# Moving the first two weight splits of a two-group encoder trunk: one behind the eviction of the modulation rows, one to GpSimd

## The chip, the cores and the metric

The kernel runs on one core of one Trainium2 chip. The metric is the device time of one execution in microseconds (us); lower is better. Engines are named as in the profile: PE is TensorE (PEld its weight loads), DVE is VectorE, ACT is ScalarE, POOL is GpSimd, SP is the engine whose queue issues the DMAs. "L543" is line 543 of the kernel before.

## The reference, cut to what matters

Two request groups of 512 tokens by 1024 features each go through the same two-layer encoder trunk. Each layer normalises, mixes and adds; only the start of layer 0 matters here.

```python
def trunk(x, c, g_norm, w_ada, b_ada, g_final, even_p, odd_p):
    for l in range(DEPTH):
        mod = jax.nn.silu(c) @ w_ada[l] + b_ada[l]
        shift, scale, gate = jnp.split(mod, 3, axis=-1)
        h = rmsnorm(x, g_norm[l]) * (1 + scale[:, None, :]) + shift[:, None, :]
        ...
        out = even_mixer(h, ...)          # layer 0: begins with u = h @ w_in0
        x = x + gate[:, None, :] * out
    return rmsnorm(x, g_final)
```

So before the first large product `h @ w_in0` can start, the kernel needs the modulation rows (`mod`), the norm of x, and h made from both.

## The kernel before

**Number format.** All large products are done in three passes to keep float32 accuracy: a weight block w is split into `w_hi` (w rounded to the type fp32r) and `w_lo` = w - `w_hi`, the activations likewise into `h_hi` and `h_lo`, and PE does `w_hi*h_hi`, `w_hi*h_lo`, `w_lo*h_hi` (L561, L562, L563 in `three`). The weights come as 81 blocks of 128 x 1024 per group. SP loads them into a ring of three slots (`wring`, L556); for each block ACT rounds it (`act_split`, L531, semaphore `w_hi`) and DVE subtracts (`dve_split`, L543, semaphore `w_lo`), into two pairs of buffers. PE waits on `w_lo` before it uses a block (`wait_split`), and SP loads block n+3 once `w_lo` has counted n+1.

**The prologue.** Before the first block, DVE and PE fold small weights together (`expand` L441, `keep` L446 to L448, `fold` L368 to L372), PE accumulates the modulation rows of the first of three parts over eight steps (`ada_step`, L303) as their weights arrive, ACT squares x (L637), POOL adds the squares (`n_gpsimd`, L644 and L647), PE sums them over partitions (L652) and ACT makes `rstd` (L658, L660). Then ACT rounds the weight blocks 0 and 1 (L531).

**The end of the prologue on DVE, in program order.** `ada_evict` copies the modulation rows out of the accumulator bank (L319); `ada_add` waits for four transposes of them on PE (L311), adds the bias (L328) and makes the two scale rows (L334, twice). Then `dve_h` makes h in eight chunks of 128 x 512: for chunk c an instruction at L588 (x times scale times `rstd`, semaphore `h_scaled`), on ACT the rounding and shift (`act_h`, L599, semaphore `h_hi`), on DVE again the low half (L593, semaphore `h_lo`). The order is: L588 of chunk c, then L593 of chunk c-1. `dve_h` takes a table `splits`, by which the split of block 0 stands ahead of chunk 1 and that of block 1 ahead of chunk 2:

```python
        groups[0].dve_h(dve, 0, 0, h_A, xT, splits={1: 0, 2: 1})
```

**What PE does first.** `pe_project_two` works on blocks 0 and 1 together, in 16 steps of three matmuls. The steps are (block 0, chunk 0), (1, 0), (0, 1), (1, 1) and so on to chunk 5, then (0, 6), (0, 7), (1, 6), (1, 7). Chunk k waits for `h_lo` of that chunk; chunk 0 of block 0 waits for `w_lo` to count 1, chunk 0 of block 1 for 2. After that the blocks are done one by one; the block after next is split by ACT when a block is done.

**Orders.** Each engine runs a program of its own, written out by hand, and they meet only at semaphores. POOL's program is `n_gpsimd`, then `a_gpsimd` of group 0, whose first wait is for the constants and the bias tables.

Of the kernel before, what the change touches and what calls it, by code (L numbers as in the profile page):

```python
# [5 lines left out]
F32 = mybir.dt.float32  # L6
F32R = mybir.dt.float32r
ALU = mybir.AluOpType
# [36 lines left out]
for _n, _w in (("ident", P), ("blk", 32), ("ones", P), ("mf", 1), ("mb", 1), ("eps", 1), ("one", 1), ("mhalf", 1), ("pad", 3),  # L45
# [13 lines left out]
SLOTS = 3  # L59
PAIRS = 2  # L60
# [11 lines left out]
    up_in=32, w_lo=81, x_back=16, x_gfin=8, x_out=16, x_upd=16, y_hi=8, y_lo=8, z_bias=0, z_in0=128, z_in1=128, z_norm=3,  # L72
    z_out0=128, z_out1=128, z_sg=16)

Group = namedtuple("Group", "a_sync a_gpsimd a_tensor a_scalar a_vector e_sync e_gpsimd e_tensor e_scalar e_vector act_split dve_split stream_weights"
                           " dve_h act_h n_square n_gpsimd n_tensor n_rstd fin_tensor fin_rstd fin_scale fin_out")


# [5 lines left out]
def trunk(nc, xs, rows_in, fold_in, w_ada, blocks_in, up_q, up_kv, rpb_pad, const_in, out):  # L84
# [7 lines left out]
    def sem(name):  # L92
        if name not in sems:
            sems[name] = nc.alloc_semaphore(name)
        return sems[name]
# [7 lines left out]
    def take(n, at=None):  # L103
        lo = free[0] if at is None else at
        if at is None:
            free[0] += (n + 7) // 8 * 8
        assert lo + n <= 53200, (lo, n)
        return nc.alloc_sbuf_tensor_at(f"at_{lo}_{n}", [P, n], F32, offset=arena_at + 4 * lo)[:, :]

    def chunks(ap, w):  # L110
        return ap.rearrange("p (c w) -> p c w", w=w)

    def take_r(name, n, at=None):

        lo = free[0] if at is None else at
        if at is None:
            free[0] += n
        assert lo + n <= 53200, (name, lo, n)
        return nc.alloc_sbuf_tensor_at(name, [P, n], F32R, offset=arena_at + 4 * lo)[:, :]
# [3 lines left out]
    def cst(name, rows=P):  # L123
        a, b = CONST[name]
        return const[0:rows, a:b]
# [13 lines left out]
    xT = chunks(take(DC * T), T)  # L139
# [4 lines left out]
    whi = take_r("w_hi", PAIRS * DC * P).rearrange("p (s k n) -> p s k n", s=PAIRS, k=DC)  # L144
    wlo = take_r("w_lo", PAIRS * DC * P).rearrange("p (s k n) -> p s k n", s=PAIRS, k=DC)
    ring_lo = free[0]
    wring = take(SLOTS * DC * P).rearrange("p (s k n) -> p s k n", s=SLOTS, k=DC)
# [18 lines left out]
    def pair(name, hi_at, lo_at, n=DC):  # L166
        return (chunks(take_r(name + "_hi", n * T, at=hi_at), T), chunks(take_r(name + "_lo", n * T, at=lo_at), T))
# [57 lines left out]
    h_A = pair("h_a", Q0, K0)  # L225
# [36 lines left out]
    def ps(n):  # L262
        return PS[n // 2][:, n % 2 * T:n % 2 * T + T]
# [19 lines left out]
    groups = []  # L283
# [30 lines left out]
    def ada_evict(dve, p):  # L314

        dve.wait_ge(sem("ada_used"), DC * (p + 1))
        if p:
            dve.wait_ge(sem("ada_T"), p)
        dve.tensor_copy(ada_rows, ps(ADA_BANK[p])).then_inc(sem("ada_ev"), 1)  # L319

    def ada_add(dve, p):

        dve.wait_ge(sem("ada_T"), p + 1)
        lo = VA["bada"][0] + 2 * DC * p
        o = mod.rearrange("p l c g -> p (l c) g")[:, 2 * DC * p:2 * DC * (p + 1)].rearrange("p (q n) g -> p q n g", q=4)
        src = ps(TURN_BANK[p]).rearrange("p (n q r) -> p q n r", n=4, q=4)[:, :, :, 0:G]
        bias = vecA[:, lo:lo + 2 * DC].rearrange("p (q n) -> p q n", q=4).unsqueeze(3).to_broadcast([P, 4, 4, G])
        dve.tensor_tensor(o, src, bias, ALU.add).then_inc(sem("mod_set"), 1)  # L328
        if p != 1:
            l = p // 2  # L330
            dve.wait_ge(sem("mod_set"), 5 if l else 1)
            at_gn = VA["gn"][0] + DC * l
            for g in range(G):
                dve.scalar_tensor_tensor(scl[:, l, :, g], mod[:, l, DC:2 * DC, g], 1.0, vecA[:, at_gn:at_gn + DC], ALU.add, ALU.mult)\  # L334
                    .then_inc(sem("mod_set"), 1)
# [93 lines left out]
    def p_vector(dve):  # L429

        dve.memset(ps(ADA_BANK[0]), 0.0).then_inc(sem("p_zero"), 1)
        dve.memset(Weff.rearrange("p c x -> p (c x)"), 0.0).then_inc(sem("p_zero"), 1)
        dve.wait_ge(sem("p_vecT"), 1)
        dve.tensor_copy(vecA, ps(0)[:, 0:P]).then_inc(sem("p_vec"), 1)
        dve.tensor_copy(vecB, ps(0)[:, P:2 * P]).then_inc(sem("p_vec"), 1)
        blk = cst("blk").unsqueeze(2).to_broadcast([P, 32, 4])

        def expand(c):
            for w in range(3):
                a = Araw[:, w, c, :].unsqueeze(1).to_broadcast([P, 32, 4])  # L440
                dve.tensor_tensor(X[:, w, c, :].rearrange("p (n i) -> p n i", i=4), a, blk, ALU.mult).then_inc(sem("p_X"), 1)  # L441

        def keep(c):
            dve.wait_ge(sem("p_fold"), c + 1)
            b = ps(FOLD_BANKS[c])
            dve.tensor_copy(Gt[:, c], b[:, 0:P]).then_inc(sem("p_folded"), 1)  # L446
            dve.tensor_copy(BDv[:, c], b[:, P:2 * P]).then_inc(sem("p_folded"), 1)
            dve.tensor_copy(Weff[:, 2 * c:2 * c + 2, 0:16], b[:, 2 * P:2 * P + 32].rearrange("p (a n) -> p a n", a=2))\  # L448
                .then_inc(sem("p_folded"), 1)

        dve.wait_ge(sem("p_raw"), 16)
        dve.tensor_copy(bif, fold_src[:, FOLD_BIF:FOLD_W])
        dve.wait_ge(sem("p_zero"), 2)
        for c in range(6):
            expand(c)
        for c in range(F_LATE):
            keep(c)
            if c + 6 < IC:
                expand(c + 6)
        ada_evict(dve, 0)  # L460
        ada_add(dve, 0)
        dve.wait_ge(sem("mod_set"), 3)
        dve.wait_ge(sem("rstd_done"), 1)
        groups[0].dve_h(dve, 0, 0, h_A, xT, splits={1: 0, 2: 1})

    def by_col(ap):

# [44 lines left out]
    def group(g):  # L512
# [20 lines left out]
        def dve_split(dve, b):  # L533

            n = B_END * g + b
            if n >= B_END * G:
                return
            dve.wait_ge(sem("w_hi"), n + 1)
            if b == B_KR:
                dve.tensor_tensor(whi[:, n % PAIRS, :, ROPE:2 * ROPE], wring[:, n % SLOTS, :, 0:ROPE],  # L540
                                  whi[:, n % PAIRS, :, 0:ROPE].bitcast(F32), ALU.subtract).then_inc(sem("w_lo"), 1)
                return
            dve.tensor_tensor(wlo[:, n % PAIRS], wring[:, n % SLOTS], whi[:, n % PAIRS].bitcast(F32), ALU.subtract)\  # L543
                .then_inc(sem("w_lo"), 1)

        def pair_of(b):

            return (B_END * g + b) % PAIRS
# [278 lines left out]
        def a_vector(dve):  # L827

            for b in range(B_OUT0):
# [13 lines left out]
                if B_NAQK <= b < B_NAV:  # L843
# [7 lines left out]
                    else:  # L851
                        dve.tensor_tensor(nak[1][:, n - 4], ps(b % 4), nak[0][:, n - 4].bitcast(F32), ALU.subtract)\
                            .then_inc(sem("naqk_lo"), 1)
                dve_split(dve, b + PAIRS)
                if B_GATE + 1 <= b < B_GATE + 5:
                    for e in range(2):
# [1042 lines left out]
        def e_vector(dve):  # L1899
# [168 lines left out]
            for b in range(B_TAIL + 2, B_END):  # L2068
# [7 lines left out]
                if half:  # L2076
# [1 line left out]
                    dve.scalar_tensor_tensor(xT[:, j], ps(j), mod[:, 1, 16 + j, g:g + 1], xT[:, j],  # L2078
                                             ALU.mult, ALU.add).then_inc(sem("x_upd"), 1)

        return Group(a_sync, a_gpsimd, a_tensor, a_scalar, a_vector, e_sync, e_gpsimd, e_tensor, e_scalar, e_vector, act_split, dve_split,
                     stream_weights, dve_h, act_h, n_square, n_gpsimd, n_tensor, n_rstd, fin_tensor, fin_rstd, fin_scale, fin_out)

    groups.extend(group(g) for g in range(G))
    LAST = groups[G - 1]

    with nc.Block() as block:

        @block.sync
        def _(sp):  # L2090
            p_sync(sp)
            for group_ in groups:
                group_.a_sync(sp)
                group_.e_sync(sp)
            for j in range(DC):
                LAST.fin_out(sp, j)
            sp.wait_ge(sem("y_out"), 16 * DC * G)

        @block.gpsimd
        def _(pool):  # L2100
            groups[0].n_gpsimd(pool)
            for group_ in groups:
                group_.a_gpsimd(pool)
                group_.e_gpsimd(pool)

        @block.tensor
        def _(pe):
            p_tensor(pe)
            for group_ in groups:
                group_.a_tensor(pe)  # L2110
                group_.e_tensor(pe)
            LAST.fin_tensor(pe, 6)

        @block.scalar
        def _(act):
            p_scalar(act)
            for group_ in groups:
                group_.a_scalar(act)
                group_.e_scalar(act)
            LAST.fin_rstd(act, 6)  # L2120

        @block.vector
        def _(dve):
            p_vector(dve)
            for group_ in groups:
                group_.a_vector(dve)
                group_.e_vector(dve)
            for j in range(DC):
                LAST.fin_scale(dve, j)
# [143 lines left out]
```

## Time and profile before

| what | value |
|---|---|
| median of 3 runs | 1488.36 us (1488.08 to 1489.69) |
| time of the profiled execution | 1488.46 us |
| its span, first to last instruction | 1486.4 us |
| mean granted PE clock | 0.997 |
| PE busy | 1449.8 us (98%) |
| DVE busy | 854.4 us (57%) |
| ACT busy | 669.9 us (45%) |
| POOL busy | 365.2 us (25%) |

Times within the profile are us from the start of the span. An instruction's row gives its start, its duration, the engine, the line and the operands; in square brackets stands how long the engine had been idle before it and what released it. Instructions follow each other on an engine a little before the end of the one ahead as it is shown, since they are pipelined.

### The profile page before, as it was taken

The numbers are of one execution on the slowest core, as the hardware profiler recorded it, in microseconds if no ns is written. First come the engines' busy times: TensorE is split into PE (matmuls) and PEld (weight loads), VectorE is DVE, ScalarE is ACT, GpSimd is POOL, SyncE is SP. The second block draws the span as 40 slices with busy tenths as digits, with TensorE's granted clock in tenths as the row PEclk, the third lists the DMA queues.
The fourth block names the chain that finished last, engine by engine and source line by source line (L and its number), as shares of the span: only waits on it lengthen the run. The fifth ranks groups of instructions, "written<-read, shape, count | busy, mean of one in ns | idle before, by whom it ended". The sixth has DMA issues, their size and how long they took to land.

```text
span 1486.4 us, 18893 instructions
## 1 busy us (share of the span) xinstructions
PE 1449.8 (98%) x7162; PEld 1115.2 (75%) x7162; DVE 854.4 (57%) x1523; ACT 669.9 (45%) x1161; POOL 365.2 (25%) x455
## 2 busy tenths in 40 slices
PE   8999999999999999999999999999999999999997
PEld 5677765678787787787888887567878778787885
DVE  7523345655797427885443434566689652789423
ACT  3323446744443435543543343765444343555332
POOL 2011023421100022765210002342120002376311
PEclk9999999999999999999999999999999999999999
DMA  9566732214333331116334544222433333111531
GB/s 385 203 221 214 256 128 86 58 57 142 107 99 100 95 111 57 44 29 240 88 97 160 133 119 111 96 58 58 142 111 100 95 107 106 50 43 31 183 99 71
DMA packets 54618, 174.27 MB, mean 117 GB/s; under 512 B 6000, under 2 KB 7408, under 8 KB 52224
## 3 DMA queue, kind: packets, MB, share of 16 engines
q1 hardware_dynamic: 54528, 173.07, 36.0%
q8 instruction: 57, 0.93, 0.3%
q14 instruction: 33, 0.27, 0.1%
HBM read 149.94 MB, written 23.10 MB: 116 GB/s over the span
## 4 chain that ended last, share of the span: by engine, by line
PE 82%; DVE 8%; ACT 4%; DMA 2%; issue 2%; POOL 1%; SPq 0%; DVEq 0%; ACTq 0%; POOLq 0%
PE ps L561 21%; PE ps L563 21%; PE ps L562 21%; PE ps L1115 3%; PE ps L1151 2%; PE ps L1170 2%; PE ps L1658 1%; PE ps L1641 1%; DVE w_lo L543 1%; PE ps L303 1%; PE ps L1692 1%; PE ps L1189 1%; PE ps L1482 1%; PE ps L1132 1%; DMA at<-z_kept 1%
## 5 line engine op out<-in xcount | busy, mean ns | idle before, releaser
L543 DVE TENSOR_TENSOR w_lo<-at,w_hi 128x1024 fp32r<-128x1024 f32 x160 | 199.1, 1244 | 345.2 <-ACT w_hi L531 345.1
L531 ACT ACTIVATE w_hi<-at 128x1024 fp32r<-128x1024 f32 x162 | 169.5, 1047 | 140.1 <-PE ps L563 130.6
L561 PE MATMUL ps<-h_e_hi,w_hi 128*128 128x512 f32 x464 | 182.8, 394 | 5.0 <-DVE w_lo L543 5.0
L563 PE MATMUL ps<-h_e_hi,w_lo 128*128 128x512 f32 x464 | 180.6, 389 | 0.0
L562 PE MATMUL ps<-h_e_lo,w_hi 128*128 128x512 f32 x464 | 180.6, 389 | 0.0
L561 PE MATMUL ps<-h_a_hi,w_hi 128*128 128x512 f32 x384 | 153.7, 400 | 1.6 <-DVE h_a_lo L593 1.0
L562 PE MATMUL ps<-h_a_lo,w_hi 128*128 128x512 f32 x384 | 150.1, 391 | 0.0
L563 PE MATMUL ps<-h_a_hi,w_lo 128*128 128x512 f32 x384 | 150.0, 391 | 0.0
L561 PEld LDWEIGHTS ps<-h_e_hi,w_hi 128*128 128x128 f32 x464 | 87.1, 188 | 28.8 <-issue 8.7
L563 PEld LDWEIGHTS ps<-h_e_hi,w_lo 128*128 128x128 f32 x464 | 87.1, 188 | 18.3
L562 PEld LDWEIGHTS ps<-h_e_lo,w_hi 128*128 128x128 f32 x464 | 87.1, 188 | 18.0 <-issue 0.5
L1300 POOL TENSOR_SCALAR at<-at,at 128x256 f32<-128x256 f32 (+1 forms) x128 | 76.0, 611 | 98.9 <-DVE at L1250 98.9
L561 PE MATMUL ps<-u_h_hi,w_hi 128*128 128x512 f32 x256 | 100.2, 391 | 0.0
L563 PE MATMUL ps<-u_h_hi,w_lo 128*128 128x512 f32 x256 | 99.6, 389 | 0.0
L562 PE MATMUL ps<-u_h_lo,w_hi 128*128 128x512 f32 x256 | 99.6, 389 | 0.0
L1468 DVE SCALAR_TENSOR_TENSOR at<-ps,at,at 128x510 f32<-128x510 f32 (+1 forms) x128 | 95.9, 749 | 4.5
L561 PEld LDWEIGHTS ps<-h_a_hi,w_hi 128*128 128x128 f32 x384 | 72.4, 188 | 29.8 <-issue 12.0
L1569 POOL TENSOR_TENSOR at<-at,at 128x512 f32<-128x512 f32 x16 | 22.2, 1412 | 284.9 <-DMA at<-a_rows 284.9
L563 PEld LDWEIGHTS ps<-h_a_hi,w_lo 128*128 128x128 f32 x384 | 72.4, 188 | 15.4
L562 PEld LDWEIGHTS ps<-h_a_lo,w_hi 128*128 128x128 f32 x384 | 72.5, 189 | 14.8 <-issue 0.7
L573 POOL TENSOR_TENSOR at<-at,at 128x512 f32<-128x512 f32 x25 | 38.1, 1525 | 138.1 <-ACT at L1895 95.0
L1234 DVE TENSOR_REDUCE at<-ps 128x2 f32<-128x1024 f32 x32 | 39.2, 1225 | 42.8 <-PE ps L1115 42.8
(289 smaller groups left out, 3007.0 us busy)
## 6 DMA issues: line engine op xcount, KB each, us to landing
at<-blocks_in SPq DMA_DIRECT2D x162, 512.0 KB, 3.8
at<-w_ada SPq DMA_DIRECT2D x32, 512.0 KB, 4.6
at<-w_ada SPq DMA_DIRECT2D x8, 1024.0 KB, 17.7
at<-xs SPq DMA_DIRECT2D x4, 2048.0 KB, 10.7
z_kept<-at SPq DMA_DIRECT2D x32, 256.0 KB, 2.1
at<-z_kept SPq DMA_DIRECT2D x32, 256.0 KB, 2.7
sg_kept<-at SPq DMA_DIRECT2D x16, 256.0 KB, 4.5
at<-sg_kept SPq DMA_DIRECT2D x16, 256.0 KB, 2.6
```

Source lines behind the costliest of these rows:

```text
L531: act.activation(whi[:, n % PAIRS, :, cols], wring[:, n % SLOTS, :, cols], ACT.Copy).then_inc(sem("w_hi"), 1)
L543: dve.tensor_tensor(wlo[:, n % PAIRS], wring[:, n % SLOTS], whi[:, n % PAIRS].bitcast(F32), ALU.subtract)\
L561: pe.matmul(o, stationary[0], moving[0], start=first, stop=False)
L562: pe.matmul(o, stationary[0], moving[1], start=False, stop=False)
L563: return pe.matmul(o, stationary[1], moving[0], start=False, stop=final)
L573: pool.tensor_tensor(acc, acc, sqb[:, c % 2], ALU.add).then_inc(sem("sq_added"), 1)
L1115: last = pe.matmul(ps(s_bank(j) + e), qcat[0:QK, u, m * P:(m + 1) * P], kcat[0:QK, u], start=True, stop=True)
L1151: last = pe.transpose(ps(4 + q)[:, col:col + P], Pt[:, j % 4, m, k * P:(k + 1) * P], ident)
L1170: last = pe.matmul(ps(6 + n % 2)[64 * e:64 * e + 64, 2 * P * half:2 * P * half + 2 * P], vmla[:, s, 2 * n + e], PT[(j - 1 + e) % 4][:, 2 * ...
L1234: dve.tensor_reduce(nmx[:, 2 * i:2 * i + 2], ps2(i % 2).rearrange("p (e t) -> p e t", e=2), AX.X, ALU.max, negate=True).then_inc(sem("c_ma ...
L1300: last = pool.tensor_scalar(p, p, rinv[:, n:n + 1], 1.0, ALU.mult, ALU.mult)
L1468: dve.scalar_tensor_tensor(y[:, lo:hi], src[:, lo + d:hi + d], vb("convw", t * IC + c), y[:, lo:hi], ALU.mult, ALU.add).then_inc(sem("e_co ...
```

## The change

Block 0 is now split on DVE directly behind the eviction of the modulation rows, ahead of the bias add. Block 1 is split by POOL, with the same subtraction of a 128 x 1024 block, behind the norm's additions and ahead of the bias tables; POOL waits for `w_hi` to count 2 and for `w_lo` to count 1. `dve_h` no longer holds any split. Later splits stay as they were.

```diff
         ada_evict(dve, 0)
+        groups[0].dve_split(dve, 0)
         ada_add(dve, 0)
         dve.wait_ge(sem("mod_set"), 3)
         dve.wait_ge(sem("rstd_done"), 1)
-        groups[0].dve_h(dve, 0, 0, h_A, xT, splits={1: 0, 2: 1})
+        groups[0].dve_h(dve, 0, 0, h_A, xT)
...
+        def pool_split(pool, b):
+
+            pool.wait_ge(sem("w_hi"), b + 1)
+            pool.wait_ge(sem("w_lo"), b)
+            pool.tensor_tensor(wlo[:, b % PAIRS], wring[:, b % SLOTS], whi[:, b % PAIRS].bitcast(F32), ALU.subtract)                .then_inc(sem("w_lo"), 1)
...
         @block.gpsimd
         def _(pool):
             groups[0].n_gpsimd(pool)
+            groups[0].pool_split(pool, 1)
             for group_ in groups:
                 group_.a_gpsimd(pool)
                 group_.e_gpsimd(pool)
```

(The rest of the diff adds `pool_split` to the tuple of functions that `group` returns.)

## Rows read from the trace of the kernel before

**Rows 1.** The page, part 1: busy time and share of the span.
```profile
PE 1449.8 (98%) x7162; PEld 1115.2 (75%) x7162; DVE 854.4 (57%) x1523; ACT 669.9 (45%) x1161; POOL 365.2 (25%) x455
```

**Rows 2.** Chain that ended last, around 37: start, us, what.
```profile
37.01 1.13 DVE w_lo L543
```

**Rows 3.** Timeline of DVE: start, us, engine, line, operands, idle before.
```profile
34.19 0.69 DVE L319 COPY at<-ps 128x512 f32<-128x512 f32 x1 [0.41 <-PE ps L303]
35.75 0.19 DVE L328 TENSOR_TENSOR at<-ps,at 128x32 f32<-128x32 f32 x1 [0.87 <-PE ps L311]
35.98 0.24 DVE L334 SCALAR_TENSOR_TENSOR at<-at,at 128x8 f32<-128x8 f32 x2
36.26 0.75 DVE L588 SCALAR_TENSOR_TENSOR at<-at,at,at 128x512 f32<-128x512 f32 x1
36.92 1.22 DVE L543 TENSOR_TENSOR w_lo<-at,w_hi 128x1024 fp32r<-128x1024 f32 x1
38.06 0.74 DVE L588 SCALAR_TENSOR_TENSOR at<-at,at,at 128x512 f32<-128x512 f32 x1
38.72 0.74 DVE L593 SCALAR_TENSOR_TENSOR h_a_lo<-at,at,h_a_hi 128x512 fp32r<-128x512 f32 x1
39.38 1.22 DVE L543 TENSOR_TENSOR w_lo<-at,w_hi 128x1024 fp32r<-128x1024 f32 x1
40.52 0.74 DVE L588 SCALAR_TENSOR_TENSOR at<-at,at,at 128x512 f32<-128x512 f32 x1
41.18 0.74 DVE L593 SCALAR_TENSOR_TENSOR h_a_lo<-at,at,h_a_hi 128x512 fp32r<-128x512 f32 x1
...
48.42 1.63 DVE L593 SCALAR_TENSOR_TENSOR h_a_lo<-at,at,h_a_hi 128x512 fp32r<-128x512 f32 x2
```

**Rows 4.** Timeline of ACT, same stretch.
```profile
33.77 1.06 ACT L531 ACTIVATE w_hi<-at 128x1024 fp32r<-128x1024 f32 x1 [3.21 <-DMA at<-blocks_in]
35.06 1.06 ACT L531 ACTIVATE w_hi<-at 128x1024 fp32r<-128x1024 f32 x1 [0.23 <-DMA at<-blocks_in]
37.04 0.72 ACT L599 ACTIVATE h_a_hi<-at,at 128x512 fp32r<-128x512 f32 x1 [0.93 <-DVE at L588]
```

**Rows 5.** Timeline of PE, first three-pass products.
```profile
39.61 0.76 PE L561 MATMUL ps<-h_a_hi,w_hi 128*128 128x512 f32 x1 [0.98 <-DVE h_a_lo L593]
...
42.31 0.45 PE L561 MATMUL ps<-h_a_hi,w_hi 128*128 128x512 f32 x1
...
52.05 0.39 PE L563 MATMUL ps<-h_a_hi,w_lo 128*128 128x512 f32 x1
...
54.83 0.39 PE L561 MATMUL ps<-h_a_hi,w_hi 128*128 128x512 f32 x1
...
64.80 0.39 PE L563 MATMUL ps<-h_a_hi,w_lo 128*128 128x512 f32 x1
```

**Rows 6.** Windows: stretch, us, busy PE PEld DVE ACT POOL, clock, DMA share, GB/s.
```profile
38.10:38.70 0.60, 0.53 (x5) 0.43 (x4) 0.60 (x2) 0.00 (x0) 0.00 (x0) 1.00 0.15 62
38.70:39.60 0.90, 0.00 (x0) 0.02 (x1) 0.90 (x3) 0.72 (x1) 0.00 (x0) 0.68 0.88 153
39.60:42.30 2.70, 2.69 (x6) 2.04 (x7) 2.67 (x4) 1.00 (x4) 0.00 (x0) 0.50 0.63 208
```

**Rows 7.** Timeline of POOL and of DVE near 696.
```profile
695.90 1.29 POOL L1588 TENSOR_TENSOR at<-at,at 128x512 f32<-128x512 f32 x1 [0.20 <-DMA at<-z_kept]
696.16 2.12 DVE L543 TENSOR_TENSOR w_lo<-at,w_hi 128x1024 fp32r<-128x1024 f32 x1 [1.78 <-ACT w_hi L531]
```

**Rows 8.** Windows of L441 alone: stretch, us, busy DVE, clock, DMA share, GB/s.
```profile
17.09:19.57 2.48, 2.48 (x3) 1.00 1.01 420
...
26.88:27.56 0.68, 0.68 (x3) 1.00 1.02 422
```

**Rows 9.** Groups of POOL by shape, and its timeline at 93.
```profile
L1560 POOL TENSOR_TENSOR xc_g_lo<-at,xc_g_hi 128x512 fp32r<-128x512 f32 x32 | 41.1, 1284 | 2.6
```
```profile
93.53 1.33 POOL L761 TENSOR_TENSOR at<-at,at 128x256 f32<-128x256 f32 x2 [8.25 <-DMA t_masked<-at]
```

More of the change, by code:

```diff
@@ L73 @@
     z_out0=128, z_out1=128, z_sg=16)
-Group = namedtuple("Group", "a_sync a_gpsimd a_tensor a_scalar a_vector e_sync e_gpsimd e_tensor e_scalar e_vector act_split dve_split stream_weights"
+Group = namedtuple("Group", "a_sync a_gpsimd a_tensor a_scalar a_vector e_sync e_gpsimd e_tensor e_scalar e_vector act_split dve_split pool_split stream_weights"
                            " dve_h act_h n_square n_gpsimd n_tensor n_rstd fin_tensor fin_rstd fin_scale fin_out")
@@ L2079, in e_vector @@
                                              ALU.mult, ALU.add).then_inc(sem("x_upd"), 1)
-        return Group(a_sync, a_gpsimd, a_tensor, a_scalar, a_vector, e_sync, e_gpsimd, e_tensor, e_scalar, e_vector, act_split, dve_split,
+        return Group(a_sync, a_gpsimd, a_tensor, a_scalar, a_vector, e_sync, e_gpsimd, e_tensor, e_scalar, e_vector, act_split, dve_split, pool_split,
                      stream_weights, dve_h, act_h, n_square, n_gpsimd, n_tensor, n_rstd, fin_tensor, fin_rstd, fin_scale, fin_out)
```

## The prediction

> **What bounds the kernel now.** I read the page first: PE is busy in 98% of the span [rows 1], so the time moves only where PE waits or runs at its lower clock. Then the chain of waits: nearly all of it is the three-pass matmuls, and at the end of the prologue it leaves PE for DVE, through the split of block 0 [rows 2]. The edit is all in that place, so I read the timelines of DVE, ACT and PE from 34 to 53. The reader is to see four things.
>
> First, DVE is idle for 0.87 between the eviction, which ends at 34.88, and the bias add at 35.75, and there is no idle time on it from there to 50.05 that matters [rows 3]: 34.88 to 35.75 is the hole in which the first split is to go. Second, the rounded block 0 is there at 33.77 + 1.06 = 34.83 and block 1 at 36.12 [rows 4]. Third, PE stands idle for 0.98 before its first three-pass matmul at 39.61, 0.15 behind the first `h_lo` (38.72 + 0.74 = 39.46) [rows 3, 5]. Fourth, PE's granted clock falls in that hole, from 1.00 to 0.50, the lower of its two levels (1.2 against 2.4 GHz), and stays there to about 42.3 [rows 6]: the first six matmuls of the pair take 42.31 - 39.61 = 2.70, 0.45 each, and the other 42 take 52.28 - 42.31 = 9.97 [rows 5], where 52.28 is the last start plus 0.23. In block 2's even stretch the 4th starts at 54.83 and the 48th at 64.80, 44 steps of 0.2266 [rows 5], which makes 9.52 for 42; the missing 0.45 is waiting for DVE, whose last `h_lo` comes at 50.05, with nine matmuls (2.23) behind it.
>
> **The change part by part.**
>
> *Two splits leave `dve_h`.* Each costs DVE 1.14 there (36.92 to the next start, 38.06; 39.38 to 40.52) [rows 3]. That alone would bring the last `h_lo` 2.28 earlier.
>
> *Split of block 0 behind the eviction.* It needs the rounded block 0, there at 34.83, and DVE, free at 34.88 [rows 3, 4]: from 34.88 to 36.10 (1.22). The bias add behind it can start at about 36.02 in place of 35.75: +0.27. The hole hides 0.87 of the 1.14. PE's four transposes wait for the eviction only and don't move. The cover is thin: the block is there 0.05 before it is needed, where it had 36.92 - 34.83 = 2.09 to spare; whatever the block lands later is now paid in full (third rival).
>
> *Split of block 1 on POOL.* The trace has no POOL subtraction of 128 x 1024. The nearest is L1560, the same operation with the same output type on 128 x 512, 1.284; the bias tables at 256 columns take 1.33 for two, 0.67 each [rows 9]. The slope between them is (1.284 - 0.67)/256, 2.4 ns a column, so 1024 columns come to 1.284 + 512 x 0.0024 = 2.51. Bounds: 2 x 1.284 = 2.57, and 4.3 if it is held up as much in proportion as DVE's split there [rows 7] was (2.12 for 1.22, 2.5 x 1.74). I take 2.5. It starts when `w_lo` counts 1 (36.10) and `w_hi` 2 (36.12); ACT starts 0.03 behind a DVE release (37.04 behind 37.01) [rows 3, 4], so I put POOL at 36.15 to 36.2, and its end at 38.7. Behind it in POOL's queue stand only the bias tables, whose data SP asks for no sooner than at its fifth block, long after: free. PE needs this half only three matmuls after its first: also free. SP issues block 3 behind the first split, which ends at 36.10 in place of 38.14, and block 4 behind the second, 38.7 in place of 40.60 [rows 3]; neither block is needed before the pair and block 2 are through PE, so nothing is gained or lost.
>
> *What POOL's split does to DVE.* This is the price that decides. POOL runs a two-input add from 695.90 to 697.19 [rows 7]; DVE's split, the same that takes 1.22 elsewhere, starts at 696.16 and ends at 698.28, 1.09 behind POOL's end: DVE did nothing while POOL ran. The multiplies of the prologue say it again: three `expand` multiplies take 0.68 together when POOL is quiet and 2.48 when POOL adds squares [rows 8], 1.80 of waiting. So a DVE instruction with two operands in SBUF waits out a POOL instruction that started first. In the changed kernel DVE issues such instructions from 36.25 on (L334 takes `mod` and the norm weights; L588 takes x and `rstd`), POOL starts at 36.15 to 36.2, and all of DVE stands until 38.7. The bias add of L328 has one operand in PSUM and is through by 36.2.
>
> The Trainium skill ("SBUF — State Buffer", "Who interferes with whom") states the same as a rule: the shared port pair is an exclusive lock, a DVE instruction with two SBUF inputs contends with a GpSimd instruction that reads SBUF, and whoever issues first makes the other block fully. By that rule the sum is the one below; by its absence the first rival's. On the size of POOL's part the skill ("GPSIMD Engine Reference", "Performance versus the Vector engine") gives 4497 ns for a tensor_tensor add of 2048 columns; half of that, an estimate, is 2.25, and the stall would be 0.25 shorter. The rows of this kernel, 1.284 for 512, decide for 2.5.
>
> *The sum on DVE.* POOL ends at 38.7. The two L334 are through by 38.9, and L588 of chunk 0 starts at 38.93 (36.26 before). L588 of chunk 1 follows 0.66 later, at 39.6. ACT rounds chunk 0 from 38.93 + 0.75 + 0.03 = 39.71 to 40.43; L593 of chunk 0 waits for that and runs from 40.46 to 41.20. So the first `h_lo` comes at 41.20, 1.74 later than 39.46. L588 of chunk 2 starts at 41.24 in place of 40.52, and from there the rhythm is that of before: each further `h_lo` is 0.72 later, the last at 50.77. In short: +0.27 for what of split 0 sticks out of the hole, +2.4 for the stall, -2.28 for the two splits, and +0.3 since L593 of chunk 0 now waits for ACT, which the split of block 0 used to cover.
>
> *The sum on PE.* Its folds still end at 38.6. It starts at 41.20 + 0.15 = 41.35, idle 2.7 where it was 0.98. The clock falls in the hole as before. If it comes back as long after PE's restart as in the rows (2.70), six matmuls run to 44.05 and 42 at 0.2266 to 53.6; DVE is ahead throughout (the 40th matmul, which needs the last `h_lo`, would start at 51.6, after 50.77). Before it was 52.28: +1.3. If the clock comes back at the same moment as before, 42.3, DVE's last `h_lo` sets the end: 50.77 + 2.23 = 53.0, +0.7. I take +1.3, since the row at the lower level shows PE at work for nearly all of it [rows 6]; the +0.7 is the lower end.
>
> Everything later hangs on this: the next block's ACT split waits for the first block's end, DVE's for that, PE for that, and the prologue's end is not hidden behind any load. So the +1.3 goes through to the end, and nothing else in the program changes. Span 1486.4 + 1.3 = 1487.7; the profiled execution's time of 1488.46 would become 1489.8, and against the median of 1488.36, 0.10 below that execution, I forecast 1489.7.
>
> **The rivals.** About 0.2%, 3.0 us, is what a measurement here can tell from no change.
>
> *POOL and DVE run side by side (other sign, faster).* Place: DVE from 36.2 to 38.7. Without the stall L588 of chunk 0 starts at 36.53, the first `h_lo` comes at 38.80, the last at 48.4, PE starts at 38.95: 38.95 + 2.70 + 9.52 = 51.2, so -1.1 and 1487.3. It decides if POOL's instruction delays DVE by less than 1.1 of its 2.5. For it: nothing but that POOL might be woken late, and even then one L588 gets ahead of it and the others wait. Against it: [rows 7, 8]. I give it 0.10.
>
> *The clock stays low for longer (slower).* PE's hole is 2.7 in place of 0.98. Each us more at 1.2 GHz costs 1 - 0.2266/0.45 = 0.50, 0.45 being the slow step above. If the low stretch behind the restart is 4.4, +0.8 more, so +2.1 and 1490.5; twice the row, 5.4, gives +2.6 and 1491.0. It passes 0.2% only if the low level holds for 6.1 behind the restart. For it: the stall itself; against: the row shows one rise and no case of a longer one. 0.17, of it 0.03 beyond +3.0.
>
> *The blocks land late (slower).* ACT idles for both blocks' DMAs [rows 4]; every us that block 0 lands later than here now delays the bias add and all behind it. One block's place in the queue is 1.29 (35.06 - 33.77): +1.3 on top, +2.6 and 1491.0. It decides from 0.05 on; it takes 1.7 to pass 0.2%. 0.08, of it 0.03 beyond.
>
> *The gain or loss is swallowed later* (a load or another engine is waited for anyway): 1488.4, 0.07.
>
> **How the numbers follow.** Forecast with its bounds (+0.7 to +2.1, 1489.0 to 1490.5): 0.58. The five cases make 1.00. The predicted time is 1489.7. The range takes in the side-by-side case and the two slower ones up to +2.9: 1487.2 to 1491.3; outside it I leave some 0.10 and the scatter of the runs, of which three spread over 1.6. Faster by over 0.2% (below 1485.4) no case gives: 0.03 for what I haven't seen. Slower by over 0.2% (above 1491.3): 0.03 + 0.03, and 0.02 for a slower POOL instruction (4.3 in place of 2.5 makes 1.3 + 1.8 = +3.1): 0.08. Within: 0.89.
>
> **What the profile after would show.** A DVE split at 34.9 and the bias add near 36.0; one POOL subtraction at 36.2, 2.5 long; behind it an L334 or L588 on DVE whose duration is stretched by the overlap; the first L593 near 40.5 and the last ending near 50.8; PE idle for about 2.7 before its first L561 at 41.3; the last matmul of the pair at about 53.4. Wrong would be: L588 at its 0.75 within POOL's instruction (then faster), a low clock beyond 45, or a w_hi of block 0 later than the eviction.

## The result, and the profile after

The changed kernel takes 1491.3 us (median of 22 runs, 1489.0 to 1497.58); the kernel before takes 1488.57 (22 runs beside them, 1487.03 to 1491.12). The ratio is 1.0016, 95% interval 1.001 to 1.0023: slower by 2.4 us, clear of zero (1.5 to 3.4), and less than the 0.2% (3.0 us) that was named as the bound of "no change", though the interval reaches past it. The profiled execution took 1490.73, with a span of 1488.9 against 1486.4.

The timeline of DVE after, at the end of the prologue (columns as ahead of the prediction; L588 is now L595, L593 is L600, L543 is L544, and the three matmuls are L568 to L570):

```profile
34.07 0.69 DVE L319 COPY at<-ps 128x512 f32<-128x512 f32 x1 [0.41 <-PE ps L303]
34.68 1.22 DVE L544 TENSOR_TENSOR w_lo<-at,w_hi 128x1024 fp32r<-128x1024 f32 x1
35.81 0.18 DVE L328 TENSOR_TENSOR at<-ps,at 128x32 f32<-128x32 f32 x1
36.03 2.41 DVE L334 SCALAR_TENSOR_TENSOR at<-at,at 128x8 f32<-128x8 f32 x2
38.48 1.42 DVE L595 SCALAR_TENSOR_TENSOR at<-at,at,at 128x512 f32<-128x512 f32 x2
40.02 0.75 DVE L600 SCALAR_TENSOR_TENSOR h_a_lo<-at,at,h_a_hi 128x512 fp32r<-128x512 f32 x1
40.80 0.75 DVE L595 SCALAR_TENSOR_TENSOR at<-at,at,at 128x512 f32<-128x512 f32 x1
...
48.72 1.63 DVE L600 SCALAR_TENSOR_TENSOR h_a_lo<-at,at,h_a_hi 128x512 fp32r<-128x512 f32 x2
```

The timeline of POOL, and of ACT, in the same stretch:

```profile
36.04 2.38 POOL L551 TENSOR_TENSOR w_lo<-at,w_hi 128x1024 fp32r<-128x1024 f32 x1 [10.95 <-DVE w_lo L544]
```
```profile
32.97 1.06 ACT L532 ACTIVATE w_hi<-at 128x1024 fp32r<-128x1024 f32 x1 [2.53 <-DMA at<-blocks_in]
34.26 1.06 ACT L532 ACTIVATE w_hi<-at 128x1024 fp32r<-128x1024 f32 x1 [0.23 <-DMA at<-blocks_in]
39.26 1.39 ACT L606 ACTIVATE h_a_hi<-at,at 128x512 fp32r<-128x512 f32 x2 [3.94 <-DVE at L595]
```

The two L334 of 128x8, which took 0.24 [rows 3], take 2.41, from 36.03 to 38.44. POOL's subtraction runs from 36.04 to 38.42: 0.02 from end to end, though neither waits for a semaphore of the other there. Taken apart, the first L334, whose record starts 0.01 ahead of POOL's, takes 0.17 as before; the second, from 36.11 to 38.44, is the one that stands.

PE's timeline at the first, seventh and last matmul of the pair, and the windows around its hole (columns as before):

```profile
40.91 0.76 PE L568 MATMUL ps<-h_a_hi,w_hi 128*128 128x512 f32 x1 [2.41 <-DVE h_a_lo L600]
...
43.61 0.50 PE L568 MATMUL ps<-h_a_hi,w_hi 128*128 128x512 f32 x1
...
53.02 0.39 PE L570 MATMUL ps<-h_a_hi,w_lo 128*128 128x512 f32 x1
```
```profile
38.50:40.40 1.90, 0.01 (x1) 0.00 (x0) 1.77 (x3) 1.14 (x2) 0.00 (x0) 1.00 0.93 272
40.40:43.60 3.20, 2.69 (x6) 2.15 (x7) 3.13 (x5) 1.94 (x6) 0.00 (x0) 0.50 0.30 118
```

PE idles for 2.41 in place of 0.98 [rows 5], and six matmuls run at the lower clock, as before; the low stretch itself is 3.4 long in both traces. To compare kernels whose prologues end some tenths apart, I take the distance from the start of the eviction (L319) to the start of the pair's last matmul: 52.05 - 34.19 = 17.86 before [rows 3, 5], 53.02 - 34.07 = 18.95 after, +1.09.

That is not the whole of +2.4. I followed the start of each block's split through both traces. The shift is +0.98 behind the pair (53.67 against 52.69) and +1.31 at 188; +0.38 at 349, and -0.13 at 912. Between 188 and 349 the profile of before was long by chance: all 13 other profiles made here are 0.1 to 1.3 shorter there. For the 0.5 between 349 and 912 I have no account. Then, in the attention of group 2, nothing of which was edited, it jumps to +2.52 at 1027 and stays near there to the end (+2.22). At that place stand DVE's timeline and POOL's, of the kernel before and then of the changed one:

```profile
918.63 0.68 DVE L973 TENSOR_TENSOR at<-ps,at 32x512 f32<-32x512 f32 x1 [4.99 <-DMA sg_kept<-at]
...
920.05 0.70 DVE L977 TENSOR_TENSOR at<-at,at 32x512 f32<-32x512 f32 x1
```
```profile
918.92 2.97 POOL L1000 TENSOR_TENSOR at<-at,at 128x512 f32<-128x512 f32 x2 [107.61 <-ACT at L951]
```
```profile
918.56 0.68 DVE L980 TENSOR_TENSOR at<-ps,at 32x512 f32<-32x512 f32 x1 [5.05 <-DMA sg_kept<-at]
...
919.99 1.64 DVE L984 TENSOR_TENSOR at<-at,at 32x512 f32<-32x512 f32 x1
```
```profile
918.56 2.52 POOL L1007 TENSOR_TENSOR at<-at,at 128x512 f32<-128x512 f32 x2 [107.39 <-DMA sg_kept<-at]
```

This is the rotary step. (The view names ACT's L951 as what released POOL before. By the program POOL's first product waits for the stored transfers and for the first of the two L947, and L951 is no part of that.) DVE makes two products and their sum (L977, now L984), which is the rotated k; POOL makes two cosine products (L1000, now L1007). Before, POOL starts 0.29 behind DVE, so its first product ends behind the start of DVE's sum, and the sum gets in between POOL's two. After, POOL starts together with DVE, its second product is ahead of the sum, and the sum takes 1.64. This lateness goes on over DVE and ACT to the first exponentials, and PE's waits and clock (views: waits of PE, 915 to 955; windows) become, first the wait before, then wait and window after:

```profile
PE ps L1115 <- ACT at L1285: 0.7, 1, 0.7
```
```profile
PE ps L1122 <- ACT at L1292: 1.8, 1, 1.8
```
```profile
938.00:941.30 3.30, 3.30 (x9) 0.52 0.00 0
```

So there are 1.1 of waiting and then a stretch of 3.4 at the lower clock. The split at the end of group 2's attention, before and after:

```profile
1026.80 1.23 DVE L543 TENSOR_TENSOR w_lo<-at,w_hi 128x1024 fp32r<-128x1024 f32 x1 [0.40 <-ACT w_hi L531]
```
```profile
1029.32 1.23 DVE L544 TENSOR_TENSOR w_lo<-at,w_hi 128x1024 fp32r<-128x1024 f32 x1 [0.40 <-ACT w_hi L532]
```

From DVE's first rotary product to that split it is 1026.80 - 918.63 = 108.17 before and 1029.32 - 918.56 = 110.76 after: +2.6.

### The profile page after: what moved, and what is told of

It reads as the page before. It is cut to its first block, busy times and chain, and to the rows that moved or that the text cites. A ratio compares the mean times of both kernels' runs of the same rounds, so it can differ in the third digit from the quotient of the medians.

```text
span 1488.9 us, 18894 instructions
## 1 busy us (share of the span) xinstructions
PE 1449.3 (97%) x7162; PEld 1116.6 (75%) x7162; DVE 853.9 (57%) x1522; ACT 669.3 (45%) x1161; POOL 368.6 (25%) x456
## 4 chain that ended last, share of the span: by engine, by line
PE 82%; DVE 9%; ACT 4%; DMA 2%; issue 2%; POOL 1%; SPq 0%; DVEq 0%; ACTq 0%; POOLq 0%
PE ps L568 21%; PE ps L570 21%; PE ps L569 21%; PE ps L1122 3%; PE ps L1158 2%; PE ps L1177 2%; DVE w_lo L544 1%; PE ps L1665 1%; PE ps L1648 1%; PE ps L303 1%; PE ps L1699 1%; PE ps L1196 1%; PE ps L1489 1%; PE ps L1139 1%; ACT w_hi L532 1%
## 5 line engine op out<-in xcount | busy, mean ns | idle before, releaser
L544 DVE TENSOR_TENSOR w_lo<-at,w_hi 128x1024 fp32r<-128x1024 f32 x159 | 197.8, 1244 | 344.3 <-ACT w_hi L532 344.2
L568 PE MATMUL ps<-h_e_hi,w_hi 128*128 128x512 f32 x464 | 182.7, 394 | 4.7 <-DVE w_lo L544 4.7
L570 PE MATMUL ps<-h_e_hi,w_lo 128*128 128x512 f32 x464 | 180.6, 389 | 0.0
L568 PE MATMUL ps<-h_a_hi,w_hi 128*128 128x512 f32 x384 | 153.5, 400 | 3.1 <-DVE h_a_lo L600 2.4
L570 PE MATMUL ps<-h_a_hi,w_lo 128*128 128x512 f32 x384 | 150.0, 391 | 0.0
L568 PEld LDWEIGHTS ps<-h_e_hi,w_hi 128*128 128x128 f32 x464 | 87.1, 188 | 28.4 <-issue 8.3
L570 PEld LDWEIGHTS ps<-h_e_hi,w_lo 128*128 128x128 f32 x464 | 87.1, 188 | 18.2
L568 PE MATMUL ps<-u_h_hi,w_hi 128*128 128x512 f32 x256 | 100.2, 391 | 0.0
L570 PE MATMUL ps<-u_h_hi,w_lo 128*128 128x512 f32 x256 | 99.6, 389 | 0.0
L568 PEld LDWEIGHTS ps<-h_a_hi,w_hi 128*128 128x128 f32 x384 | 72.5, 189 | 30.3 <-issue 12.5
L570 PEld LDWEIGHTS ps<-h_a_hi,w_lo 128*128 128x128 f32 x384 | 72.4, 188 | 15.4
L1122 PE MATMUL ps<-at,at 96*128 96x512 f32 x128 | 61.9, 606 | 3.1 <-ACT at L1292 3.1
```

The source lines that it names most:

```text
L568: pe.matmul(o, stationary[0], moving[0], start=first, stop=False)
L570: return pe.matmul(o, stationary[1], moving[0], start=False, stop=final)
L1122: last = pe.matmul(ps(s_bank(j) + e), qcat[0:QK, u, m * P:(m + 1) * P], kcat[0:QK, u], start=True, stop=True)
```

## The experiments

Theory at the start: POOL's split makes DVE stand (1.1 at the start), and the 2.6 of group 2 come from the same port, for a reason still to be found. Rivals: the cost at the start comes from putting a split ahead of the bias add; the loss of group 2 is chance, or follows from any later start. "Distance" is the one above, "group 2" the stretch that was 108.17. "Low at the pair" is the length of the low-clock stretch that falls on the pair, though some of them begin ahead of it; "low in group 2" is the same inside group 2's stretch. Edits are shown against the changed kernel; those of before_delayed, pool_tiny and before_ordered against the kernel before. In the runs block1_pool_only and after_filled the profiled execution had PE at its lower clock or waiting for 4 to 14 us in the prologue, ahead of the eviction, so of these two only the distance, group 2 and the median are used.

| kernel | distance | group 2 | low at the pair | low in group 2 | median, before beside it | ratio, 95% |
|---|---|---|---|---|---|---|
| before | 17.86 | 108.17 | 3.4 | none | 1488.57 | |
| changed | 18.95 | 110.76 | 3.4 | 3.4 | 1491.3, 1488.57 | 1.0016 (1.001 to 1.0023) |
| after_again | 20.23 | 110.75 | 6.8 | 3.4 | 1492.13, 1488.68 | 1.0014 (0.9997 to 1.003) |
| block0_only | 17.11 | 108.79 | none | none | 1487.67, 1488.93 | 0.9987 (0.997 to 1.0003) |
| block1_pool_only | 20.56 | 109.27 | 6.8 | none | 1493.15, 1488.93 | 1.003 (1.0018 to 1.0042) |
| pool_twice | 21.57 | 109.17 | 6.8 | none | 1492.86, 1488.93 | 1.0034 (1.0021 to 1.0047) |
| before_delayed | 20.33 | 108.21 | 6.8 | none | 1490.65, 1488.93 | 1.0017 (1.0002 to 1.0032) |
| both_behind | 18.59 | 108.23 | 3.4 | none | 1488.67, 1488.68 | 0.9993 (0.9977 to 1.0009) |
| after_filled | 18.27 | 112.40 | none | 6.8 | 1491.14, 1488.68 | 1.0015 (0.9991 to 1.0039) |
| block0_pool | 17.82 | 112.38 | none | 6.8 | 1490.73, 1488.68 | 1.0003 (0.9987 to 1.0019) |
| pool_tiny | 17.97 | 110.79 | 3.4 | 3.4 | 1491.46, 1488.04 | 1.0013 (1.0004 to 1.0023) |
| after_ordered | 19.23 | 108.42 | 3.4 | none | 1489.81, 1488.04 | 1.0009 (0.9999 to 1.0019) |
| before_ordered | 17.87 | 108.39 | 3.4 | none | 1488.37, 1488.04 | 1.0005 (0.9995 to 1.0016) |
| block0_ordered | 17.42 | 108.35 | 3.4 | none | 1487.66, 1488.04 | 0.9996 (0.9986 to 1.0006) |

**block0_only.**
```diff
-        groups[0].dve_h(dve, 0, 0, h_A, xT)
+        groups[0].dve_h(dve, 0, 0, h_A, xT, splits={2: 1})
...
-            groups[0].pool_split(pool, 1)
```


> Block 0 is split behind the eviction, block 1 is back on DVE ahead of chunk 2, POOL has no split. I measure from the start of the eviction (L319) to the start of the last matmul of the first pair: 17.86 us before, 18.95 after the change. If POOL's port is what costs (my theory): L588 of chunk 0 starts 0.27 later than before, the first h_lo comes at 38.8 and the last 0.7 earlier than before, so the distance is 17.2 and the time 0.7 below the kernel before. If the cost came from putting a split ahead of the bias add (rival), the distance is over 17.9. If any shift of the prologue brings a further loss in group 2 (second rival, for the 1.7 us by which the median moved more than this stage), the time is above the kernel before although the distance is below.

Distance 17.11, 0.75 below before; PE's hole is 0.24 and its clock doesn't fall. The first rival falls: a split ahead of the bias add is a gain. Group 2 is 0.6 over before's with the sum in its old order, for which I have no account. The median is 1.3 below before, with an interval that ends at 1.0003.

**block1_pool_only.**
```diff
         ada_evict(dve, 0)
-        groups[0].dve_split(dve, 0)
...
-        groups[0].dve_h(dve, 0, 0, h_A, xT)
+        groups[0].dve_h(dve, 0, 0, h_A, xT, splits={1: 0})
```


> Block 1 is on POOL, block 0 is split on DVE ahead of chunk 1 as before. POOL can start when that split ends, some 2 us later than in the changed kernel, in the middle of the L588 and L593 instructions. Theory (a two-input instruction waits for POOL's): one of them is stretched by up to 2.4, and since one DVE split (1.14) is saved the distance from eviction to the last matmul of the pair is 18.9 to 19.2 (1.0 to 1.3 over before). Rival without a lock: 16.7 to 17.2, since DVE has 1.14 less to do.

POOL's and DVE's timelines:

```profile
42.34 2.72 POOL L550 TENSOR_TENSOR w_lo<-at,w_hi 128x1024 fp32r<-128x1024 f32 x1 [17.07 <-DVE w_lo L543]
```
```profile
42.77 2.83 DVE L599 SCALAR_TENSOR_TENSOR h_a_lo<-at,at,h_a_hi 128x512 fp32r<-128x512 f32 x1
```

One L593 (here L599) takes 2.83 in place of 0.75 and ends 0.54 behind POOL: the stall follows POOL's instruction to where it is. POOL's own instruction takes 2.72 here in place of 2.38. The distance, 20.56, is 1.4 above my upper value; the lower clock held for 6.8, which I had not reckoned with.

**pool_twice.**
```diff
             pool.wait_ge(sem("w_lo"), b)
+            pool.tensor_tensor(...).then_inc(sem("dup"), 1)
+            pool.wait_ge(sem("dup"), 1)
             pool.tensor_tensor(...).then_inc(sem("w_lo"), 1)
```
(The two additions have the same operands, which are left out here.)

> As the changed kernel, but POOL makes the split of block 1 twice, one behind the other. Theory: DVE's L334 and L588 wait for both, so the first h_lo comes 2.4 later, the distance from eviction to the last matmul of the pair goes from 18.95 to about 21.3 and the time rises by 2.3 over the changed kernel. Rival (DVE waits for something else): the w_lo of block 1 is needed 4 us after POOL's start in the changed kernel, so a second pass of 2.4 is hidden but for some tenths; distance below 19.4. If DVE gets in between POOL's two instructions, an L334 or L588 lies there and the stall is in two pieces of the same sum.

DVE's and POOL's timelines:

```profile
35.78 2.41 DVE L334 SCALAR_TENSOR_TENSOR at<-at,at 128x8 f32<-128x8 f32 x2
38.23 3.57 DVE L597 SCALAR_TENSOR_TENSOR at<-at,at,at 128x512 f32<-128x512 f32 x2
```
```profile
35.79 2.38 POOL L551 TENSOR_TENSOR w_lo<-at,w_hi 128x1024 fp32r<-128x1024 f32 x1 [10.97 <-DVE w_lo L544]
38.25 2.34 POOL L553 TENSOR_TENSOR w_lo<-at,w_hi 128x1024 fp32r<-128x1024 f32 x1
```

Each POOL instruction stops DVE once: L334 behind the first, the pair of L588 (here L597), 3.57 in place of 1.42, behind the second. The first `h_lo` is complete 8.85 after the eviction's start, 6.70 in the changed kernel: +2.15 for 2.34 more of POOL. The distance is 2.6 longer, in part by the longer low stretch. This shows POOL's instruction as the cause of the stall at the start; by what path it stops DVE no row shows, but block0_pool below shows which operands matter. L588's record starts 0.02 ahead of POOL's second and it waits all the same: where the two start within some hundredths, the starts don't tell which will wait.

In group 2 POOL's second product is ahead of DVE's sum here too (the sum takes 1.63) and PE waits 1.8, but the clock stays up:

```profile
938.00:941.30 3.30, 2.35 (x7) 1.00 0.00 0
```

Group 2 is 109.17, and 109.27 in block1_pool_only, which has no low stretch there either. So the late sum by itself costs 1.0 to 1.1. Where a low stretch of 3.4 follows, the stretch is 110.75 to 110.79 (three profiles), where one of 6.8 follows, 112.38 and 112.40: each 3.4 at the lower clock adds 1.6. Five of the seven profiles in which POOL's second product is ahead of the sum have one; what decides it isn't shown.

**before_delayed.**
```diff
                 if c in splits:
+                    if splits[c] == 1 and g == 0:
+                        dve.wait_ge(sem("w_hi"), 2)
+                        dve.tensor_tensor(wlo[:, 1], wring[:, 1], whi[:, 1].bitcast(F32), ALU.subtract).then_inc(sem("dup"), 1)
+                        dve.wait_ge(sem("dup"), 1)
```


> The kernel before, with the split of block 1 made twice on DVE, no POOL in it: a pure delay of DVE by 1.2. The first h_lo is unchanged, the others come 1.2 later, and DVE sets the end of the pair: distance 19.0 in place of 17.86, about the same as in the changed kernel. If what the changed kernel loses beyond this stage comes from the shift alone, this kernel loses it too and stands 2.5 to 3 above before; if it is a matter of the one stage, 1.2 above.

The distance is 20.33, not 19.0: I had left out that PE's second step waits for `w_lo` of block 1, which made a second hole of 1.34, and the lower clock held for 6.8. So it shifts what follows by more than the changed kernel does. Group 2 is 108.21 all the same: a later start alone doesn't bring the loss there. The median is 1.7 above before (1.0002 to 1.0032).

**after_again.** No edit.

> The changed kernel itself, once more, for a second profile of it beside the others. The stage at the start should be 18.95 again. In the first profile the attention of group 2 lost 2.65 near 936 to 941, where PE waited 1.80 for ACT's L1292 (0.72 before) and fell to its lower clock. If that belongs to the change it is there again; if it is chance it may be absent.

Group 2 is 110.75, as in the first profile to 0.01: it belongs to the change. The distance is 20.23; DVE's times are those of the first profile to 0.01 (first `h_lo` complete 6.69 after the eviction's start), but the lower clock holds for 6.8 in place of 3.4:

```profile
39.60:46.40 6.80, 5.68 (x14) 0.50 0.22 80
```

So 1.28 of scatter lies in the clock alone, with the same kernel.

**both_behind.**
```diff
         groups[0].dve_split(dve, 0)
+        groups[0].dve_split(dve, 1)
...
-            groups[0].pool_split(pool, 1)
```


> Both splits on DVE behind the eviction, POOL has none. The bias add comes at 37.3 in place of 35.75 (+1.5), dve_h is 2.28 shorter, the first h_lo 0.6 later and the last 0.4 earlier than before; PE starts at about 40.2 and 48 matmuls with six slow ones end 0.1 later than before: distance 17.9 to 18.0, against 18.95 with POOL's split. That is the price of POOL as against DVE for the same work in the same place: 1.0. If POOL's instruction cost DVE nothing, this kernel would be the slower one by 1.1.

Distance 18.59, 0.6 more than expected: here the clock fell late, at 41.5, with PE at work, and 3.4 of the pair ran at the lower one. The first `h_lo` is complete 6.07 after the eviction's start, 0.8 later than before (0.6 expected) and 0.63 earlier than with POOL's split. The median is that of before. DVE alone does the same two splits in the same place for 0.63 less on the first `h_lo` than DVE and POOL together.

**after_filled.**
```diff
         for c in range(F_LATE + 1, IC):
             fold(c)
+        pe.wait_ge(sem("w_hi"), 1)
+        for _ in range(10):
+            pe.matmul(ps(7), whi[:, 0, 0], whi[:, 0, 0:4], start=True, stop=True)
```


> The changed kernel, with ten extra three-pass-sized matmuls (128x512) on PE into an unused bank between the last fold and the first pair, so PE works through its 2.4 us hole. If the six slow matmuls are due to that hole, the clock stays at 1.00, the pair is bound by DVE, whose last h_lo comes at 50.3, and the distance falls from 18.95 to 18.3 to 18.4. If the clock falls in spite of it, 18.9 to 19.0. The first h_lo and POOL's stall don't move.

This kernel adds work whose result nobody uses. The granted clock is 1.00 from where the hole was through the pair, and the distance is 18.27, as expected: 0.68 of the 1.09 is the lower clock that follows the hole. The other 0.41 is DVE's: the last `h_lo` ends 16.28 after the eviction's start, in the changed kernel too, and 15.86 before. It is one profile, but none of the five with a hole of 2.4 or more and nothing in it kept its clock. The time doesn't show it (group 2 at 112.40).

**block0_pool.**
```diff
         ada_evict(dve, 0)
-        groups[0].dve_split(dve, 0)
...
-        groups[0].dve_h(dve, 0, 0, h_A, xT)
+        groups[0].dve_h(dve, 0, 0, h_A, xT, splits={2: 1})
...
-            groups[0].pool_split(pool, 1)
+            groups[0].pool_split(pool, 0)
...
                 if c in splits:
+                    dve.wait_ge(sem("w_lo"), 1)
```
(`pool_split` waits for `w_lo` only if b is not 0.)

> The engines swapped: POOL splits block 0 as soon as it is rounded, DVE splits block 1 ahead of chunk 2 as before. POOL runs from 34.1 to 36.4 or from 34.9 to 37.3, as block 0 lands; meanwhile DVE does the eviction and the bias add, which have an operand in PSUM, and must not be delayed; L334 waits for POOL's end, by 0.4 to 1.3. dve_h is 1.14 shorter. Distance 17.3 to 18.1, thus 0.5 below to 0.3 above the kernel before. If every DVE instruction waited for POOL, the eviction or the bias add would be stretched to POOL's end.

POOL's timeline and DVE's:

```profile
34.47 2.36 POOL L551 TENSOR_TENSOR w_lo<-at,w_hi 128x1024 fp32r<-128x1024 f32 x1 [9.40 <-ACT w_hi L531]
```
```profile
34.05 0.69 DVE L319 COPY at<-ps 128x512 f32<-128x512 f32 x1 [0.41 <-PE ps L303]
35.61 0.19 DVE L328 TENSOR_TENSOR at<-ps,at 128x32 f32<-128x32 f32 x1 [0.87 <-PE ps L311]
35.84 1.09 DVE L334 SCALAR_TENSOR_TENSOR at<-at,at 128x8 f32<-128x8 f32 x2
```

POOL works from 34.47 to 36.83. The eviction and the bias add, with at most one operand in SBUF, keep their 0.69 and 0.19 in the middle of it; L334, with two, takes 1.09 and ends 0.10 behind POOL. So of the DVE instructions here only those with two operands in SBUF wait for POOL. The distance, 17.82, is that of before, and yet the median is 2.0 higher, though with an interval that takes in 1: group 2 is 112.38 in the profile, with 6.8 at the lower clock. By now all six profiles with a split on POOL (of five kernels) had POOL and DVE start within 0.01 in the rotary step of group 2, and all four without it had POOL 0.28 to 0.29 later.

**pool_tiny.**
```diff
             groups[0].n_gpsimd(pool)
+            pool.wait_ge(sem("w_hi"), 2)
+            pool.wait_ge(sem("w_lo"), 1)
+            pool.memset(hln[:, 0:1], 0.0)
```


> The kernel before, with both splits on DVE where they were, but with the change's two waits on POOL and behind them a memset of 128x1 that reads nothing. In all six profiles with a split on POOL, POOL's first cosine product of group 2 starts within 0.01 of DVE's first sine-side product, in all four without it 0.29 later; where it starts together, POOL's second product gets ahead of DVE's k-rope add, which then takes 1.64 in place of 0.70, and PE later waits 1.7 to 1.8 for ACT's exponentials in place of 0.7 to 1.1. If that comes from POOL's program being longer (theory), it is here too: offset 0.00, wait 1.7 to 1.8, the distance at the start 17.9, the time 1 to 2.6 above before. If it comes from the split's work or from the later start of the products (rival), the offset is 0.29, the wait 0.7 and the time that of before.

POOL's and DVE's timelines, and PE's waits from 915 to 955:

```profile
38.73 0.10 POOL L2104 MEMSET at<- 128x1 f32 x1 [13.05 <-DVE w_lo L543]
...
918.82 2.52 POOL L1000 TENSOR_TENSOR at<-at,at 128x512 f32<-128x512 f32 x2 [107.22 <-DMA sg_kept<-at]
```
```profile
918.82 0.68 DVE L973 TENSOR_TENSOR at<-ps,at 32x512 f32<-32x512 f32 x1 [4.86 <-DMA sg_kept<-at]
...
920.25 1.65 DVE L977 TENSOR_TENSOR at<-at,at 32x512 f32<-32x512 f32 x1
```
```profile
PE ps L1115 <- ACT at L1285: 1.6, 1, 1.6
```

A memset of 0.10 and two waits, with both splits where they were, make the whole of it: offset 0.00, sum 1.65, PE's wait 1.6, group 2 at 110.79, the distance unchanged within 0.11, and a time clear of before (1.0013, 1.0004 to 1.0023). (One of its 12 runs took 1813.55, at a granted clock of 0.751; it isn't in the ratio, and its cause isn't known.) The loss in group 2 needs neither the split nor the stall, only what stands more in POOL's program.

**after_ordered, before_ordered, block0_ordered.** The same edit on the changed kernel, on the kernel before, and on block0_only:
```diff
                 pool.wait_ge(sem("b_act"), at("b_act", k + 1))
+                if k:
+                    pool.wait_ge(sem("b_kpe"), at("b_kpe", 1))
```


> The changed kernel, and in the rotary step of both groups POOL's second cosine product waits for DVE's k-rope add. If what the changed kernel loses beyond the prologue comes from POOL getting ahead there, the add takes 0.70 in both groups, PE's wait for ACT falls from 1.8 to about 0.8 in group 2, and the time falls from 2.7 above before to 1.1 or less; the prologue stays as in the changed kernel. If the loss is elsewhere, the time doesn't fall.

> The kernel before with the same order written in. Group 2 has it already by its timing; in group 1 the add takes 1.66 before, so only group 1 can gain: PE's wait there falls from 1.2 to about 0.7, the time by 0 to 0.5.

> Block 0 behind the eviction, block 1 on DVE in its old place, no split on POOL, and the order of the rotary step written in. The two gains add up if they are independent: 0.7 at the start and 0 to 0.5 in group 1, so 1487.5 to 1488.0 against 1488.7 for the kernel before. If the gain at the start is eaten by the first wait of group 1, as the drift of 0.4 near 190 hints, 1488.3 or more.

DVE's and POOL's timelines in after_ordered:

```profile
920.22 0.68 DVE L984 TENSOR_TENSOR at<-at,at 32x512 f32<-32x512 f32 x1
```
```profile
918.79 1.29 POOL L1009 TENSOR_TENSOR at<-at,at 128x512 f32<-128x512 f32 x1 [107.26 <-DMA sg_kept<-at]
921.05 1.28 POOL L1009 TENSOR_TENSOR at<-at,at 128x512 f32<-128x512 f32 x1 [0.96 <-DVE at L984]
```

POOL still starts together with DVE, but the order is held: the sum takes 0.68, PE's wait is 0.8, group 2 is 108.42, and the median is 1.8 above before in place of 2.7, where 1.1 or less was expected. The step in between is thereby shown in the profile: what cost 2.3 in group 2 (110.76 against 108.42) was the order of POOL's second product and DVE's sum, and the low stretch behind it. The times alone don't show it, as the intervals of the two ratios overlap. In group 1 the sum takes 1.65 to 1.66 in both the kernel before and the changed one, PE waits 1.2 to 1.3 for ACT, and the clock doesn't fall. On the kernel before the edit shortens that sum to 0.68, but PE's wait there goes only from 1.2 to 1.1, and in group 2 it rises from 0.7 to 0.9; the time doesn't move. block0_ordered ends at 1487.66, 0.4 below before, with an interval over 1; I don't claim a gain for it, nor for block0_only.

## Why the prediction was right, and where it was short

Forecast 1489.7 (+1.3), range 1487.2 to 1491.3; measured 1491.3, at the upper end, and +2.4 by the ratio. The side and the class of change came out. The interval of the ratio, 1.5 to 3.4, leaves out the +1.3: the sum had one of two terms. That the time still lies in the range owes something to luck. The two terms measured in the first profile, 1.1 at the start and 2.6 in group 2, make 3.7, which would be outside; other stages of that profile give back 1.4 between 188 and 912, of which 0.9 is chance in the profile of before. Of the 1.3 that was forecast, 1.1 was met by the mechanism that was named.

- *The split of block 0.* Its place is right: 34.68 to 35.90, bias add at 35.81. In the profile of the changed kernel the rounded block was there 0.65 before it was needed, so the rival of a late block had no say.
- *The size of POOL's part.* 2.38 measured, 2.51 reckoned from the rows for 512 and 256 columns. The Trainium skill's figure ("GPSIMD Engine Reference", "Performance versus the Vector engine"), halved as an estimate, was 2.25; the measured duration lies between.
- *The stall.* As forecast, with L334 as the first to wait. The rival "side by side" is out, by pool_twice and block0_pool. The rule of the Trainium skill ("SBUF — State Buffer", "Who interferes with whom") that a two-input instruction blocks against GpSimd's reads, and one with at most one SBUF input doesn't, agrees with block0_pool's rows to 0.1.
- *The sum on DVE and PE.* From the eviction's start the first `h_lo` is complete 1.43 later than before (1.74 forecast), and the pair's last matmul starts 1.09 later (1.3). The last `h_lo` is 0.42 later (0.72 forecast), and sets nothing, since PE at its lower clock is behind it. The term that I took from the lower clock, six matmuls, was met in one profile and missed in after_again, where it held for 6.8 and cost 1.28 more: the second rival, to which I gave 0.17, is a frequent case. Of the five profiles here with a hole of 2.4 or more and nothing to fill it, two have 3.4 at the lower clock in the pair and three have 6.8.
- *"Nothing else in the program changes".* This is the step that failed. The change lengthened POOL's program, and POOL's first product in group 2, 880 us later, came 0.29 earlier against DVE, which put its second ahead of DVE's sum; that cost 2.6 in both profiles of the changed kernel, 1.0 of it by the late sum and 1.6 by the low stretch that followed. My search for what is late next ended with the engines' order in the first stage.

**Open.** Why POOL starts 0.29 later in the kernels without the added instructions isn't shown. DVE's first product and POOL's are released by the same transfers, and nothing in the profile stands between. It is not the shift in time (before_delayed) and not the split's work (pool_tiny). In before_delayed, where DVE's program is the longer one, DVE's first product of group 1 starts 0.37 behind POOL's (211.70 against 211.33), while in all 13 other profiles they start together there: so it may not be a matter of POOL alone. Whether the place of the instructions in each program is what matters wasn't tried. That the low stretch after a hole varies between runs of one kernel is measured; what decides it isn't.

## What to carry to other kernels

Work that goes to POOL with operands in SBUF is not free for DVE: put it where DVE has no instructions or such with an operand in PSUM, as block0_pool did with 2.36 of POOL's time for 0.85 on DVE, and not at the head of a run of two-operand ones. Even there it gained nothing here: block0_pool's distance was that of before. Where POOL and DVE meet with such instructions in a later stage and the faster order isn't held by a semaphore, an edit to one program can flip it; compare the stages of both traces to the end before a difference of 0.2% is put down to the edit, and write the order in.

## What the runs showed of the hardware that was not expected

Two waits and a memset of 0.10 us on POOL moved its start by 0.29 against DVE's 880 us later, in every profile (ten with instructions added to POOL's program at 0.00 to 0.01, four without at 0.28 to 0.29; in before_ordered and block0_ordered the only addition ahead of the product is one wait in group 1's rotary step). And a PE hole of one and the same length (2.41 in two profiles of the changed kernel) was followed by 3.4 us at the lower clock in one and 6.8 in the other.
